# Gate steps of the SSD branch re-cut by chunks, norms taken by tiles, and lo parts issued ahead of an evacuation

## The reference, cut to what matters

```python
u = rms_norm(x, norm_w) * (1.0 + scale) + shift          # scale, shift, gate from w_ada
fq, fk, fv, ff, fg, dq, dk, dv, iq, ik, iw, dg, sz, sxbc, sdt, mg = split(u @ w_in)
fq = rms_norm(fq by heads); fk likewise                    # normed heads
dq = partial_rope(rms_norm(dq by heads)); dk likewise      # normed, turned heads
y_fox = fox_attention(fq, fk, fv, ...) * silu(fg)          # tanh gates
y_dsa = dsa_attention(dq, dk, dv, top-64 by iq, ik, iw) * silu(dg)
y = ssd_scan(conv(sxbc), ...) * silu(sz)                   # gate sz, 4 groups of 512
y_ssd = rms_norm(y by groups of 512)
merged = g0 * (y_fox @ w_o_fox) + g1 * (y_dsa @ w_o_dsa) + g2 * (y_ssd @ w_o_ssd)
x = x + gate * (merged @ w_out)
```

## Time and profile before

| | |
|---|---|
| median of 3 runs | 3412.45 us (3411.65 to 3414.31) |
| the profiled execution | 3413.68 us, of which the span is 3411.9 us |
| TensorE busy | 96% of the span |
| VectorE busy | 66% |
| ScalarE busy | 50% |
| mean granted clock of TensorE | 0.99 |
| chain that ended last | PE 85%, DVE 9%, ACT 3%, DMA 2% |

### The profile page before, as it was taken

One profiled execution on the slowest core, in us unless ns is written; L12 is line 12 of the kernel. 1 busy time (PEld: TensorE's weight loads), 2 busy tenths in 40 slices (PEclk: granted clock), 3 DMA queues, 4 the chain that ended last, 5 costly groups with the idle time before them and its releaser, 6 DMA issues.

```text
span 3411.9 us, 43404 instructions
## 1 busy us (share of the span) xinstructions
PE 3288.4 (96%) x17994; PEld 2849.1 (84%) x17994; DVE 2253.1 (66%) x2699; ACT 1702.4 (50%) x2097; POOL 46.6 (1%) x90
## 2 busy tenths in 40 slices
PE   4899999999999999999999999999999999999998
PEld 3689879788888878898898878888898899988887
DVE  7878878766676556786666566655567776544454
ACT  4455754644443445555646544334447865434343
POOL 0000000000000000000000000000000000000000
PEclk8999999999999999999999999999999999999999
DMA  9754566467777654444544567765545543455553
GB/s 403 320 189 176 199 238 254 182 227 268 262 277 290 225 207 170 172 157 161 184 174 160 183 238 270 274 236 188 195 183 191 179 167 137 165 218 197 189 190 140
DMA packets 102916, 719.29 MB, mean 211 GB/s; under 512 B 12176, under 2 KB 12256, under 8 KB 18752
## 3 DMA queue, kind: packets, MB, share of 16 engines
q1 hardware_dynamic: 93888, 675.38, 53.4%
q0 software_dynamic: 8256, 37.64, 3.1%
q10 hardware_dynamic: 576, 3.50, 0.3%
HBM read 710.08 MB, written 6.40 MB: 210 GB/s over the span
## 4 chain that ended last, share of the span: by engine, by line
PE 85%; DVE 9%; ACT 3%; DMA 2%; issue 1%; DVEq 0%; ACTq 0%
PE G L1265 78%; DVE LL L1858 3%; DMA RAW<-w_ada_turned_packed_dram 2%; PE BD L1375 1%; DVE S L2062 1%; PE BA L1402 1%; DVE RAW L1851 1%; PE BD L1437 1%; DVE RAW L1869 1%; DMA KV<-in_x_dram 1%; PE BC L1388 1%; PE BA L1456 0%; PE BC L1456 0%; PE BE L1320 0%; PE BC L1420 0%
## 5 line engine op out<-in xcount | busy, mean ns | idle before, releaser
L1497 ACT ACTIVATE HH<-RAW 128x2048 fp32r<-128x2048 f32 x546 | 1044.8, 1914 | 1077.7 <-PE G L1265 1004.4
L1858 DVE TENSOR_TENSOR LL<-RAW,HH 128x2048 fp32r<-128x2048 f32 x546 | 1248.0, 2287 | 347.1 <-ACT HH L1497 346.9
L1265 PE MATMUL G<-HH,UH 128*128 128x512 f32 x2496 | 993.8, 398 | 41.0 <-DVE LL L1858 34.9
L1265 PE MATMUL G<-LL,UH 128*128 128x512 f32 x2496 | 975.9, 391 | 0.0
L1265 PE MATMUL G<-HH,UL 128*128 128x512 f32 x2496 | 975.6, 391 | 0.0
L1265 PE MATMUL G<-UH,HH 128*128 128x256 f32 x2080 | 604.0, 290 | 13.9 <-DVE XS L2098 8.2
L1265 PEld LDWEIGHTS G<-HH,UH 128*128 128x128 f32 x2496 | 471.1, 189 | 146.4 <-DVE LL L1858 42.2
L1265 PE MATMUL G<-UL,HH 128*128 128x256 f32 x2080 | 590.9, 284 | 0.0
L1265 PE MATMUL G<-UH,LL 128*128 128x256 f32 x2080 | 590.8, 284 | 0.0
L1265 PEld LDWEIGHTS G<-LL,UH 128*128 128x128 f32 x2496 | 470.7, 189 | 100.2
L1265 PEld LDWEIGHTS G<-HH,UL 128*128 128x128 f32 x2496 | 471.6, 189 | 97.6 <-issue 2.9
(11 more groups left out here) (380 smaller groups left out, 2343.3 us busy)
## 6 DMA issues: line engine op xcount, KB each, us to landing
RAW<-in_w_in_packed_dram SPq DMA_DIRECT2D x402, 1024.0 KB, 4.8
RAW<-w_ada_turned_packed_dram SPq DMA_DIRECT2D x96, 1024.0 KB, 5.1
RAW<-in_w_out_packed_dram SPq DMA_DIRECT2D x48, 1024.0 KB, 4.8
RAW<-in_w_o_ssd_packed_dram SPq DMA_DIRECT2D x32, 1024.0 KB, 4.8
RAW<-in_w_o_fox_packed_dram SPq DMA_DIRECT2D x16, 1024.0 KB, 5.2
RAW<-in_w_o_dsa_packed_dram SPq DMA_DIRECT2D x16, 1024.0 KB, 4.9
RAW<-in_w_proj_a_packed_dram SPq DMA_DIRECT2D x16, 1024.0 KB, 4.8
RAW<-in_w_proj_b_packed_dram SPq DMA_DIRECT2D x16, 1024.0 KB, 4.8
```

Source lines behind the costliest of these rows:

```text
L1265: mm = pe.matmul(to, lt, rh, start=first, stop=end, skip_group_check=True)
L1497: a.activation(HH[g % NH][:, :n], RAW[buf(ch["f"])][:, :n], ACT.Copy).then_inc(*hi_done.up(g))
L1858: v.tensor_tensor(LL[buf(f)][:, :n], RAW[buf(f)][:, :n], HH[g % NH][:, :n].bitcast(F32), ALU.subtract).then_inc(*lo_done.up(g))
```

## The change

It has three parts.

1. **Ahead.** Blocks of normed heads (dk, dq, fq, fk) and of tanh gates (dg, fg) in the two hybrid layers are marked `ahead`. When a step of such a block is next in the evacuation lane, `slot` first puts `lo` of the newest chunk, and then the step. Before, that `lo` came behind the step, in the next `push`. All other blocks keep their order.
2. **sz.** The steps become gate0 | gate1, norm0 | norm1, turn0 | put0, turn1 | put1: one step per chunk, five in all, no half steps. The second tile has a buffer of its own (XD instead of S1) and columns of SM2 of its own. The bank pair is free from gate1's end on (`free_by`), no longer from put1's. As both tiles share the bank BE, turn1 now waits for put0.
3. **Norms.** `norm(l+1, t)` is put right behind the last `out` step of tile t, for layers 1 and 2 and for the final norm, there with the four `last` steps of that tile. A square root of one column on ACT stands ahead of the first of these `out` steps; it makes ACT load its table there. `last` of tile t waits for the last write of x of its own tile.

```diff
     def slot(self):
         self.middle()
         self.side.step(self.plan)
+        if self.evac.q and self.evac.q[0].get("ahead"):
+            self.lower()
         self.evac.step(self.plan)
+
+    def lower(self):
+        if self.low is not None:
+            self.put("lo", self.low)
+            self.low = None
...
     def push(self, ch):
         self.bring(ch)
-        if self.pend:
-            self.put("lo", self.pend[-1]["g"])
+        self.lower()
+        self.low = ch["g"]
         self.advance(1)
         self.pend.append(ch)
...
     def sz(l, g):
         def steps(b):
             o.tok_block["sz", l, g] = b
-            for t in range(2):
-                put("sz_gate", l, g, t)
-                yield
-                put("sz_norm", l, g, t)
-                yield MID
-                put("sz_turn", l, g, t)
-                yield
-                put("sz_put", l, g, t)
-                ended("sz_done", l, g, t)
+            put("sz_gate", l, g, 0)
+            yield
+            put("sz_gate", l, g, 1)
+            o.blocks[b]["free_by"] = ("sz_y", l, g, 1)
+            put("sz_norm", l, g, 0)
+            yield
+            put("sz_norm", l, g, 1)
+            put("sz_turn", l, g, 0)
+            yield
+            put("sz_put", l, g, 0)
+            put("sz_turn", l, g, 1)
+            yield
+            put("sz_put", l, g, 1)
+            ended("sz_done", l, g, 1)
         return steps
...
             for t in range(2):
                 put("out", l, jb, t)
+                if jb == 3:
+                    put("norm", l + 1, t)
+                    if l == 2:
+                        for j in range(4):
+                            put("last", t, j)
                 yield
...
-            dkv_b = o.wblock(w, DK, heads(("dk", l, 0)), u_ready, kind="tm")
-            dq_b = [o.wblock(w, DQ, heads(("dq", l, 0)), u_ready, kind="tm")]
-        dq_b.append(o.wblock(w, DQ + 512, heads(("dq", l, 1)), u_ready, kind="tm"))
+            dkv_b = o.wblock(w, DK, heads(("dk", l, 0)), u_ready, kind="tm", ahead=True)
+            dq_b = [o.wblock(w, DQ, heads(("dq", l, 0)), u_ready, kind="tm", ahead=True)]
+        dq_b.append(o.wblock(w, DQ + 512, heads(("dq", l, 1)), u_ready, kind="tm", ahead=True))
...
-            o.wblock(w, FG + j * 512, o.held(o.att_prog["fox", l][j], silu_times(("fg", l, j))), u_ready,
+            o.wblock(w, FG + j * 512, o.held(o.att_prog["fox", l][j], silu_times(("fg", l, j))), u_ready, ahead=True,
                      after=after_fg if j else None)
...
     SS = [S1, S2]
+    ZZ = [S1, XD]
...
         def sz_turn(l, g, t):
             pe.wait_ge(*sz_normed.at(l, g, t))
+            if t:
+                pe.wait_ge(*sz_done.at(l, g, 0))
...
         def out_square(l, jb, t):
             b = o.tok_block["out", l, jb]
+            if jb == 3 and t == 0:
+                a.activation(SM1[:, 60:61], EPT[:, :], ACT.Sqrt)
...
             v.wait_ge(*rstd_done.at(3, t))
             v.wait_ge(*x_back.at(2))
-            v.wait_ge(*out_x.at(2, 3, 1))
+            v.wait_ge(*out_x.at(2, 3, t))
```

More of the change, by code:

```diff
@@ L219, in gemm @@
             b["job"] = self.evac.add(job())
+            b["job"]["ahead"] = b["ahead"]
             self.user[b["set"]] = b
@@ L222, in gemm, with begin @@
                 b["after"](ch["g"])
-    def begin(self, chunks, evac, x, ready, kts, needs=None, after=None, soon=None):
+    def begin(self, chunks, evac, x, ready, kts, needs=None, after=None, soon=None, ahead=False):
         n = len(self.blocks)
         b = {"n": n, "set": n if n < 4 else n % 2, "x": x, "ready": ready, "kts": kts, "evac": evac, "chunks": chunks,
-             "needs": needs or (lambda k0: []), "after": after, "soon": soon, "job": None, "free_by": None, "end": None}
+             "needs": needs or (lambda k0: []), "after": after, "soon": soon, "ahead": ahead, "job": None, "free_by": None, "end": None}
         self.blocks.append(b)
@@ L358, in open @@
         self.pend += parts[14:]
+        self.low = 15
         self.ring = {"all": sorted(range(NR), key=lambda i: self.buf_user[i])}
@@ L519, in modulated @@
         yield
-    def norm(l):
-        for t in range(2):
-            put("norm", l, t)
     def am_first(gi):
@@ L533, in enter @@
         if gi == 0:
-            norm(l)
             put("x_keep", l)
@@ L733, in work_order @@
         o.ada["every"] = (2, 5) if l == 0 else 0
-        fx_b = [o.wblock(w, FQ + j * 512, heads(("fq", l, j)), u_ready, kind="tm") for j in range(2)]
-        fx_b += [o.wblock(w, FK + j * 512, heads(("fk", l, j)), u_ready, kind="tm") for j in range(2)]
+        fx_b = [o.wblock(w, FQ + j * 512, heads(("fq", l, j)), u_ready, kind="tm", ahead=True) for j in range(2)]
+        fx_b += [o.wblock(w, FK + j * 512, heads(("fk", l, j)), u_ready, kind="tm", ahead=True) for j in range(2)]
         fx_b += [o.wblock(w, FV + j * 512, tokens(("fv", l, j)), u_ready, kind="tm") for j in range(2)]
@@ L739, in work_order @@
         for j in range(2):
-            o.wblock(w, DG + j * 512, o.held(o.att_prog["dsa", l][j], silu_times(("dg", l, j))), u_ready)
+            o.wblock(w, DG + j * 512, o.held(o.att_prog["dsa", l][j], silu_times(("dg", l, j))), u_ready, ahead=True)
         for j in range(4):
@@ L803, in work_order @@
         o.slot()
[L804 to L807, removed]
     return o
@@ L1638, in sz_gate @@
             a.wait_ge(*multiplied(b))
-            a.wait_ge(*evac_before("sz_gate", l, g, t))
-            a.activation(S1[:, :], GB[o.blocks[b]["set"]][t][:, :], ACT.Tanh, scale=0.5).then_inc(*sz_tanh.up(l, g, t))
+            if t == 0:
+                a.wait_ge(*evac_before("sz_gate", l, g, t))
+            a.activation(ZZ[t][:, :], GB[o.blocks[b]["set"]][t][:, :], ACT.Tanh, scale=0.5).then_inc(*sz_tanh.up(l, g, t))
         def sz_norm(l, g, t):
             a.wait_ge(*sz_y.at(l, g, t))
-            a.activation(S1[:, :], xsK[:, g, t, :], ACT.Square, accum_out=SM2[:, 0:1]).then_inc(*sz_sum.up(l, g, t))
+            a.activation(ZZ[t][:, :], xsK[:, g, t, :], ACT.Square, accum_out=SM2[:, 2 * t:2 * t + 1]).then_inc(*sz_sum.up(l, g, t))
             a.wait_ge(*sz_sum.at(l, g, t))
-            a.activation(SM2[:, 1:2], SM2[:, 0:1], ACT.Sqrt, bias=EPT[:, 0:1],
+            a.activation(SM2[:, 2 * t + 1:2 * t + 2], SM2[:, 2 * t:2 * t + 1], ACT.Sqrt, bias=EPT[:, 0:1],
                          scale=1.0 / 512).then_inc(*sz_root.up(l, g, t))
@@ L2082, in sz_gate @@
             v.wait_ge(*sz_tanh.at(l, g, t))
-            v.scalar_tensor_tensor(S1[:, :], S1[:, :], 1.0, bk[:, :], ALU.add, ALU.mult).then_inc(*own.up())
+            v.scalar_tensor_tensor(ZZ[t][:, :], ZZ[t][:, :], 1.0, bk[:, :], ALU.add, ALU.mult).then_inc(*own.up())
             v.wait_ge(*own.last())
             v.wait_ge(*ssd_yd.at(l, g, 1))
-            v.scalar_tensor_tensor(y, S1[:, :], 0.5, y, ALU.mult, ALU.mult).then_inc(*sz_y.up(l, g, t))
+            v.scalar_tensor_tensor(y, ZZ[t][:, :], 0.5, y, ALU.mult, ALU.mult).then_inc(*sz_y.up(l, g, t))
         def sz_norm(l, g, t):
@@ L2090, in sz_norm @@
             v.wait_ge(*sz_root.at(l, g, t))
-            v.reciprocal(SM2[:, 1:2], SM2[:, 1:2]).then_inc(*own.up())
+            r = SM2[:, 2 * t + 1:2 * t + 2]
+            v.reciprocal(r, r).then_inc(*own.up())
             v.wait_ge(*own.last())
-            v.tensor_scalar(y, y, SM2[:, 1:2], None, ALU.mult).then_inc(*sz_normed.up(l, g, t))
+            v.tensor_scalar(y, y, r, None, ALU.mult).then_inc(*sz_normed.up(l, g, t))
         def sz_put(l, g, t):
```

## The result

The changed kernel takes 3383.78 us in the median of 4 runs (3381.92 to 3384.31), the kernel before 3412.64 beside it; the ratio is 0.9914, with a 95% interval from 0.9897 to 0.9931. The gain is 28.9 us, more than the forecast's 19.7, and inside the range. A second set of runs on another occasion gave 3382.63 and a ratio of 0.9908 (0.9891 to 0.9924). The profiled execution has a span of 3380.1 us against 3411.9, so 31.8 less; that is more than 28.9, as it is the fastest of its four, and the profiled execution of the kernel before lies 1.0 us above its median.

What follows compares the result with a forecast made beforehand. TensorE was taken as the bound, busy 3288 of 3412 us. Terms -7.4 - 2.6 - 2.0 + 0 - 2.3 - 3.4 - 2.0 = -19.7 gave 3394.0 us profiled, 3393 as median; range 3379 to 3406.

Steps and rivals of the forecast that it cites:

- more is gained: Rival for sz in layer 0: put0 in time after all (-4.9), clock never falls (-4.3): 3384 us; chance 0.12.
- the rope stretch: Behind fg in layer 1, rope-table steps delay three low parts, 6.3 us together; waits of about 4.0 stay: -2.3.
- The bound of 123 us: Whole kernel: TensorE busy 3288 of 3412 us, so at most 123 us can be won by order alone.
- Lo ahead of heads, -7.4: At heads, low part fits into VectorE's 5.14 us idle; five TensorE waits go, 5.8 + 1.6 = 7.4 us.
- The dq head: Where VectorE did not idle: rotation ends 2.3 us later, at 1388.2, still ahead of the turn at 1389.46; nothing paid.
- Turn1 behind put0, 4.9: Sz, layer 0: turn1 waits for put0 in the first two blocks, 2.6 and 2.3 us; in time in the last two.
- The rival in which turn1 waits in all eight: Rival: turn1 pays 3.0 us in each sz block, 24 instead of 4.9, plus four clock drops: 3418 us; chance 0.06.
- The chain at fg, 5.7 twice: Gemms of chunks 101 and 298 wait for the tanh gate behind high part, low part and two products: 5.7 us each.
- the 18.9 us of sz: Gemm waits at gate sz expected to go: 13.2 us in layer 0 (put1 and norm), 5.7 in layer 1 (forced).
- The clock in layer 0, -2.0: From 594 to 720 us, at most 6.3 us lost to lower clock; eight waits become three, a third regained: -2.0.
- Norms and end, -3.4 and -2.0: Two norm boundaries gain 1.7 us each by early table load and tile 0's chain; eight last steps end 2.0 earlier.
- The rival that VectorE is the limit and the waits only move: Rival, layer 0: the 8.3 and 2.0 us return, rope steps gain nothing, half the heads' gain lost: 3409 us; chance 0.08.

Runs made afterwards that it cites:

- e6: Changed kernel with put0 and put1 of sz both half a gemm after their turns and turn1 a chunk later, four steps per block: 3365.71 us, ratio 0.9862.
- e5: Changed kernel with put1 of sz half a gemm after turn1, so a block takes four chunks: 3371.86 us, ratio 0.9878.
- e1: Kernel before with only lo put ahead of heads and tanh gates, sz steps and norms as before: 3402.56 us, ratio 0.9965.

## Why the prediction was right, and where its sum was off

The direction, the mechanism and every wait that it named came out, within 15 us of the times named. The size came out less well: the time is 9 us better than the likeliest, at the value of the rival "more is gained" (3384). Only half of that rival's mechanism came about, less loss to the clock; turn1, which it had never waiting, waited. That the number agrees is chance. The terms that missed (heads, turn1, the clock, the rope stretch) all missed to the same side, so they did not cancel. The bound of 123 us for what order alone can win was no bound: it took TensorE's busy time as fixed, and that fell by 8.5.

- **Lo ahead of heads, -7.4.** All five waits are gone; the shift in the two stretches is 3.6 + 5.7 = 9.3. The dq head paid nothing, as laid out. The rest of 1.9 I cannot put down to single waits: TensorE's busy time for the same chunks is 0.9 less in each of the two stretches, and the runs don't show why.
- **Turn1 behind put0, 4.9.** It waited in two blocks of eight, as forecast, at 609 and 646: 1.74 and 1.95, where 2.6 and 2.3 had been worked out. The rival in which turn1 waits in all eight falls.
- **The chain at fg, 5.7 twice.** Measured 5.80 twice, in the order forecast. So the two waits nearly undid the 18.9 us of sz: 3.7 + 11.6 came in their place.
- **The clock in layer 0, -2.0: the first term that failed.** I took a third of the upper bound by counting waits. Busy time by stretch, columns as above, from the high part of chunk 83 to that of chunk 104, in the kernel before, the changed kernel, `e6` and `e5`:

```profile
594.96:750.51 155.55, 142.40 (x832) 126.58 (x831) 108.97 (x158) 87.59 (x122) 1.61 (x3) 0.95 0.54 200
...
590.03:736.84 146.81, 137.32 (x832) 122.40 (x831) 113.32 (x163) 79.92 (x116) 1.61 (x3) 0.97 0.57 212
...
589.86:723.65 133.79, 133.79 (x832) 120.24 (x831) 110.71 (x160) 81.83 (x118) 1.60 (x3) 1.00 0.63 232
...
591.73:730.37 138.64, 134.32 (x832) 120.01 (x831) 110.80 (x160) 81.82 (x117) 1.60 (x3) 1.00 0.61 224
```

  For the same 832 matmuls TensorE was busy 5.1 us less. Of the shift of 8.7 the waits explain 13.2 - 3.7 - 5.8 = 3.7; the other 5.0 is this busy time, in matmuls that now ran at the full clock. Against `e6`, which never waits, the eight short waits of before cost 8.6 us by what follows them: the term was -5, not -2, inside its bounds. But a count of waits gives no price: `e5` has three turn waits there, 1.7, 0.5 and 2.1, and keeps the full clock.
- **The stretch behind fg in layer 1, -2.3: the second.** I laid out 4.0 us of waits that would stay; 1.0 stayed. The rope steps were to run beside the new wait; they begin as it ends (1916.57). `e1` shows 2.5 us of it as the work of ahead, which I had credited to the heads alone. `e5` and `e6` show that the rest returns when the forced slot goes. The shift for this stretch and the sz blocks of layer 1 is 6.8; 5.3 of it are these waits, and most of the rest is TensorE's busy time, 1.6 less for the same chunks.
- **Norms and end, -3.4 and -2.0.** Each norm 5.43 to 3.88 (forecast 3.7), the end 2.2. Right.

The rival that VectorE is the limit and the waits only move falls most clearly by `e6`: with the same instructions in another order TensorE never waits there.

## What to carry to other kernels

Count the steps of an evacuation against the chunks of its block: five steps for four chunks look harmless in each block, yet where the banks are released early the lag adds up and is paid in one long wait at the first block that must have its banks back; where they are released late, it is paid in a short wait at nearly every block. A wait that an engine's order makes costs its own length and can cost a slower clock after it, so many short waits may be worth removing even where their sum is small; look at the clock behind them. A long wait hides work that comes to light when it goes. Where a step needs what another engine wrote in the step before, set them apart: with both puts half a gemm behind their turns and turn1 a chunk later, no wait of sz was left (`e6`); with put1 alone moved, the turn waits stayed (`e5`).

## What the runs showed of the hardware

In the kernel before the granted clock over the sz blocks of layer 0 was 0.95 in the mean, with eight waits of 0.7 to 2.8 us; in the changed one 0.97 with three of 1.7 to 5.8, and 1.00 with none (`e6`), but 1.00 also with three of 0.5 to 2.1 (`e5`). So waits of this length can be followed by the lower level of the clock, and need not be. In the changed kernel the clock fell to its lower level of 1.2 GHz within the wait at fg and rose 3 us after the gemm began; it fell for 3.4 us behind the turn wait of 1.95, and not at all behind that of 1.74. Busy time by stretch:

```profile
725.80:732.70 6.90, 3.07 (x7) 2.48 (x8) 6.11 (x9) 1.72 (x4) 0.00 (x0) 0.51 0.32 133
647.30:650.70 3.40, 3.40 (x10) 2.62 (x9) 1.52 (x4) 0.00 (x0) 0.00 (x0) 0.50 0.30 123
```

In the second profiled execution of the changed kernel, with the same wait of 5.8 at fg, the clock over the first of these stretches was 0.75 instead of 0.51: the same wait does not cost the same each time.
